# The low parts of a mixer's last weight tiles on VectorE alone

## The chip, the cores and the metric

The kernel runs on one core of one Trainium2 chip. The metric is the device time of one execution in microseconds (us). In the names of the profile TensorE is PE (its weight loads PEld), VectorE is DVE, ScalarE is ACT, GpSimd is POOL and SyncE is SP.

## What is computed

Two blocks follow one another on a sequence of 256 tokens of width 1024 in float32: a first one of two layers (feed-forward, dilated attention or retention, feed-forward), and a second one, also of two layers, each of a mixer and an MLP. The change is in the mixer of the second block. Its end, and what follows it, are:

```python
        gates = jax.nn.sigmoid((gate_logits + b_gate[l]).reshape(B, S, N_BRANCHES, D))
        merged = gates[:, :, 0] * y_diff + gates[:, :, 1] * y_mla + gates[:, :, 2] * y_mem
        x = x + merged @ w_out[l]

        u = rmsnorm(x, g_mlp[l]) @ w_mlp1[l]
        x = x + jnp.square(jax.nn.relu(u)) @ w_mlp2[l]
```

## The kernel before, in words

**Split products.** Every float32 product of activations and weights is made of three matmuls of rounded values: high by high, high by low, low by high. A weight tile is 128 x 1024 numbers. SP loads it from memory into one of four raw buffers (L1554), ScalarE copies it into one of four high buffers (`w_hi`, L1884), and then VectorE (L2186) or GpSimd (L2892) makes the low part, raw minus high (`w_lo`). TensorE waits for a tile's `w_lo` and then runs its 12 matmuls of 512 columns (`mm`, L1605 to L1607) or 24 of 256 columns (`mm_whole`, L1631, L1632, L1640).

**Order.** Python code writes one plan of steps, and each engine runs the steps that concern it in the plan's order, so every engine is a queue in order. When tile i has been used, `tile_used(i)` puts the step `split` of tile i + 4 into the plan. ScalarE's part of that step waits for TensorE's end of tile i, because it overwrites the same buffer. SP's part loads the tile that reuses the raw buffer, once the low part is made. Which engine makes the low part is decided when the step is written:

```python
    def split(self, i):
        self.step("split", i, "pool" if self.share and i % self.share == 0 else "dve")
```

`self.share` is 0 at the start of every stage. The mixer's step `outputs` sets it to 2 when attention begins (L1491), and the next stage, the MLP, sets it back to 0 (L663). In between, tiles with an even number have their low part made by GpSimd, the others by VectorE.

**The end of the mixer.** The last gated branches are added into `mx_merged` by VectorE (L2856, L2861: the merges). TensorE then transposes it (four groups of four, L1694), ScalarE copies the high part (`xt_hi`, L1914) and VectorE makes the low part (`xt_lo`, L2214). `last_plain` runs the output projection: eight tiles, four for columns 0 to 511 and four for columns 512 to 1023. They are called t0 to t7 here, and the first tiles of the MLP m0, m1 and so on. `hold_last` (L547) keeps back the split that t7's use would write, and those of the MLP's tiles behind it until `feed` releases them. So the steps `split` that are written while `last_plain` runs are those of t4, t5, t6, t7, m0, m1 and m2. The splits of t0 to t3 are written before it, in the merges.

**The start of the MLP.** Behind these steps `feed` (L675) writes for columns 0 to 511 and each half of the tokens: the addition of the projection to x (L2301, "add"), the product with the gain of the norm (`tok`, L2194, "gain"), and then the transposes of `tok` by TensorE, one group of four for each half ("turn", L1694). ScalarE's and VectorE's copies of them (`xt_hi`, `xt_lo`) feed the first matmuls of m0. The same for columns 512 to 1023 comes behind m0 and m1. POOL's next step then is the load of a gain (L2880).

Of the kernel before, what the change touches and what calls it, by code (L numbers as in the profile page):

```python
# [379 lines left out]
def drive(main, side=None, every=1, finish=True, steps=1):  # L380
    n = 0
    while True:
        try:
            next(main)
        except StopIteration as stop:
            result = stop.value
            break
        n += 1
        if side is not None and n % every == 0:
            for _ in range(steps):  # L390
                next(side, None)
    if side is not None and finish:
        for _ in side:
            pass
    return result


class Kernel:
# [869 lines left out]
    def mix(self, layer, _):  # L1268
# [252 lines left out]
        for c in range(2):  # L1521
            for half in range(HALVES):
                self.turn(lambda h, s: merged[:, h, s * P:(s + 1) * P], merged_t, half, [(4 * c + j, 4 * c + j) for j in range(4)],
                          [("merged", layer, half, c)], self.xt_after)
        self.tok_after = [[("turned", self.uid)]] * HALVES
        drive(self.last_plain(merged_t, a["w_out_2"][layer], D))


# [1519 lines left out]
```

## Time and profile before

| what | value |
|---|---|
| time before, median of 3 runs (lowest, highest) | 2466.48 us (2465.91, 2467.77) |
| profiled execution: its time | 2465.57 us |
| profiled execution: its span | 2464.3 us |
| TensorE clock granted, mean | 0.993 |
| busy: TensorE, VectorE, ScalarE, GpSimd | 97%, 62%, 48%, 12% |
| instructions | 34969 |

The span goes from the first to the last instruction of the profiled execution. Its time is 1.3 us longer, for what lies around the span, and 0.91 us below the median of the three runs. Busy shares are means over all ten stages. The first mixer ends near 1742 us of the span, the second near 2274 us.

### The profile page before, as it was taken

To read this page: it belongs to the slowest core of one execution; us is meant where nothing else is said; L and a number is where in the kernel's file an instruction comes from. 1 tells how busy PE (TensorE), PEld (TensorE's weight loads), DVE (VectorE), ACT (ScalarE), POOL (GpSimd) and SP (SyncE) were. 2 spreads that over 40 slices of the span, in tenths; PEclk is the share of its full clock that TensorE was granted. 3 is DMA by queue.
4 is the path that set the end of the run, shared out by engine and by line. 5 is a ranking of instruction groups with operands and counts; after the bars stand their busy time and mean duration, and the time that the engine had idled before them with its cause. 6 is when DMAs were issued, how large, how long until landed. Compare 5 with 4: busy or idle time off the path is not lost.

```text
span 2464.3 us, 34969 instructions
## 1 busy us (share of the span) xinstructions
PE 2385.3 (97%) x14214; PEld 2053.5 (83%) x14214; DVE 1522.5 (62%) x2325; ACT 1188.6 (48%) x1782; POOL 284.5 (12%) x247
## 2 busy tenths in 40 slices
PE   9998999889999999999999999999999999999999
PEld 8986777779979987777899787787898877887997
DVE  6555556666556547666665677755665577656654
ACT  4443454344435445444444464654554455554543
POOL 1100010000000000000000122333100122333000
PEclk9999999999999999999999999999999999999999
DMA  7755544446656655544566654445566554445564
GB/s 222 207 194 159 167 123 143 129 145 183 186 173 179 187 188 179 170 132 150 177 184 198 195 175 140 120 135 164 176 182 217 178 173 122 120 145 162 172 187 145
DMA packets 269424, 411.69 MB, mean 167 GB/s; under 512 B 13770, under 2 KB 141658, under 8 KB 269264
## 3 DMA queue, kind: packets, MB, share of 16 engines
q1 hardware_dynamic: 262400, 389.59, 52.1%
q0 software_dynamic: 6432, 19.28, 2.9%
q8 instruction: 112, 1.84, 0.3%
q10 hardware_dynamic: 432, 0.59, 0.1%
q14 instruction: 48, 0.39, 0.0%
HBM read 408.31 MB, written 1.10 MB: 166 GB/s over the span
## 4 chain that ended last, share of the span: by engine, by line
PE 79%; DVE 13%; ACT 5%; issue 2%; POOL 1%; DMA 0%; SPq 0%; ACTq 0%; DVEq 0%
PE banks L1605 14%; PE banks L1607 14%; PE banks L1606 14%; PE banks L1632 10%; PE banks L1631 9%; PE banks L1640 9%; DVE w_lo L2186 3%; ACT w_hi L1884 2%; PE banks L1754 1%; PE banks L1694 1%; PE banks L1707 1%; PE banks L1739 1%; DVE mx_merged L2861 1%; DVE probs L2373 1%; POOL stat L2873 1%
## 5 line engine op out<-in xcount | busy, mean ns | idle before, releaser
L2186 DVE TENSOR_TENSOR w_lo<-w_raw,w_hi 128x1024 fp32r<-128x1024 f32 x688 | 837.9, 1224 | 681.4 <-ACT w_hi L1884 678.9
L1884 ACT ACTIVATE w_hi<-w_raw 128x1024 fp32r<-128x1024 f32 (+2 forms) x744 | 776.8, 1049 | 564.3 <-PE banks L1607 413.6
L1631 PE MATMUL banks<-xt_hi,w_hi 128*128 128x256 f32 x1920 | 475.8, 282 | 12.1 <-ACT xt_hi L1914 8.9
L1632 PE MATMUL banks<-xt_hi,w_lo 128*128 128x256 f32 x1920 | 474.9, 286 | 0.0
L1605 PE MATMUL banks<-w_hi,xt_hi 128*128 128x512 f32 (+2 forms) x1088 | 447.3, 411 | 14.2 <-DVE xt_lo L2214 4.4
L1607 PE MATMUL banks<-w_hi,xt_lo 128*128 128x512 f32 (+2 forms) x1088 | 427.7, 393 | 0.0
L1606 PE MATMUL banks<-w_lo,xt_hi 128*128 128x512 f32 (+2 forms) x1088 | 427.3, 393 | 0.0
L1631 PEld LDWEIGHTS banks<-xt_hi,w_hi 128*128 128x128 f32 x1920 | 365.9, 191 | 15.9 <-issue 12.4
L1632 PEld LDWEIGHTS banks<-xt_hi,w_lo 128*128 128x128 f32 x1920 | 363.4, 189 | 0.0
L1640 PE MATMUL banks<-xt_lo,w_hi 128*128 128x256 f32 x1920 | 270.3, 283 | 0.0
L1605 PEld LDWEIGHTS banks<-w_hi,xt_hi 128*128 128x128 f32 x1088 | 206.7, 190 | 61.5 <-issue 8.1
L1640 PEld LDWEIGHTS banks<-xt_lo,w_hi 128*128 128x128 f32 x1920 | 248.6, 189 | 0.0
L1607 PEld LDWEIGHTS banks<-w_hi,xt_lo 128*128 128x128 f32 x1088 | 206.3, 190 | 47.4
L1606 PEld LDWEIGHTS banks<-w_lo,xt_hi 128*128 128x128 f32 x1088 | 206.8, 190 | 43.5 <-issue 3.1
L2873 POOL TENSOR_TENSOR stat<-stat,minus_half 128x1 f32<-128x1 f32 (+2 forms) x60 | 55.5, 931 | 1060.3 <-DVE stat L2273 712.0
L2892 POOL TENSOR_TENSOR w_lo<-w_raw,w_hi 128x1024 fp32r<-128x1024 f32 x56 | 134.5, 2401 | 277.2 <-ACT w_hi L1884 277.2
L1605 PE MATMUL banks<-w_hi,ffn_ht_hi 128*128 128x512 f32 x352 | 140.1, 398 | 0.0
L1607 PE MATMUL banks<-w_hi,ffn_ht_lo 128*128 128x512 f32 x352 | 139.1, 395 | 0.0
L1606 PE MATMUL banks<-w_lo,ffn_ht_hi 128*128 128x512 f32 x352 | 138.2, 393 | 0.0
L1607 PE MATMUL banks<-w_hi,mlp_ht_lo 128*128 128x512 f32 x256 | 101.7, 397 | 0.0
L1606 PE MATMUL banks<-w_lo,mlp_ht_hi 128*128 128x512 f32 x256 | 101.1, 395 | 0.0
L1605 PE MATMUL banks<-w_hi,mlp_ht_hi 128*128 128x512 f32 x256 | 100.9, 394 | 0.0
(398 smaller groups left out, 2824.7 us busy)
## 6 DMA issues: line engine op xcount, KB each, us to landing
w_raw<-in_w_mlp SPq DMA_DIRECT2D x128, 512.0 KB, 3.7
w_raw<-in_w_in SPq DMA_DIRECT2D x104, 512.0 KB, 3.7
w_raw<-in_ffn_w_gate SPq DMA_DIRECT2D x88, 512.0 KB, 4.1
w_raw<-in_ffn_w_up SPq DMA_DIRECT2D x88, 512.0 KB, 4.2
w_raw<-in_ffn_w_down SPq DMA_DIRECT2D x88, 512.0 KB, 3.6
w_raw<-in_attn_w_in SPq DMA_DIRECT2D x72, 512.0 KB, 3.8
w_raw<-in_ret_w_in SPq DMA_DIRECT2D x64, 512.0 KB, 3.9
w_raw<-in_ret_w_out SPq DMA_DIRECT2D x16, 512.0 KB, 3.9
```

Source lines behind the costliest of these rows:

```text
L1605: pe.matmul(bank, xh, wh, start=(c == 0), stop=False)
L1606: pe.matmul(bank, xh, wl, start=False, stop=False)
L1607: mm = pe.matmul(bank, xl, wh, start=False, stop=(c == b.chunks - 1))
L1631: pe.matmul(out[f], hi[:, cols], xh, start=(c == 0), stop=False)
L1632: pe.matmul(out[f], lo[:, cols], xh, start=False, stop=False)
L1640: mm = pe.matmul(out[f], hi[:, cols], xl, start=False, stop=(c == DC - 1))
L1694: mm = pe.transpose(bank[:, j * P:(j + 1) * P], t.src(t.half, s), order)
L1707: mm = pe.transpose(bank[0:z.shape[-1], at:at + P], z, order)
L1884: act.activation(k.w_hi[i % SPLIT][:, 0:m], k.raw[i % RAW][:, 0:m], ACT.Copy).then_inc(*ev.mark(k.w_hi_made, ("w_hi", i)))
L2186: dve.tensor_tensor(lo, raw, hi.bitcast(F32), ALU.subtract).then_inc(*ev.mark(k.w_lo_made, ("w_lo", i)))
L2873: pool.tensor_tensor(out, mean, k.minus_half[:, 0:n], ALU.pow).then_inc(*ev.mark(k.pool_done, name))
L2892: pool.tensor_tensor(lo, raw, hi.bitcast(F32), ALU.subtract).then_inc(*ev.mark(k.w_lo_pool, ("w_lo", i)))
```

## The change

The mixer sets `self.share` to 0 right before it calls `last_plain`, behind the steps of the merges and of the four transposes. The rest of the kernel is the same.

```diff
@@ -1523,6 +1523,7 @@
                 self.turn(lambda h, s: merged[:, h, s * P:(s + 1) * P], merged_t, half, [(4 * c + j, 4 * c + j) for j in range(4)],
                           [("merged", layer, half, c)], self.xt_after)
         self.tok_after = [[("turned", self.uid)]] * HALVES
+        self.share = 0
         drive(self.last_plain(merged_t, a["w_out_2"][layer], D))
```

## Rows read from the trace of the kernel before

**Rows 1.** The page, busy us, share and instructions of each engine

```profile
PE 2385.3 (97%) x14214; PEld 2053.5 (83%) x14214; DVE 1522.5 (62%) x2325; ACT 1188.6 (48%) x1782; POOL 284.5 (12%) x247
```

**Rows 2.** Windows of the first output projection: stretch, length, busy (instructions), clock, DMA, GB/s

```profile
1718.30:1730.00 11.70, 11.70 (x47) 9.43 (x46) 2.90 (x4) 3.78 (x4) 3.00 (x2) 0.89 0.21 59
1730.00:1742.00 12.00, 12.00 (x53) 9.62 (x52) 5.37 (x6) 4.25 (x4) 5.56 (x3) 1.00 0.63 196
```

**Rows 3.** Groups by line: low parts on GpSimd, and on VectorE by shape

```profile
L2892 POOL TENSOR_TENSOR w_lo<-w_raw,w_hi 128x1024 fp32r<-128x1024 f32 x56 | 134.5, 2401 | 277.2 <-ACT w_hi L1884 277.2
...
L2186 DVE TENSOR_TENSOR w_lo<-w_raw,w_hi 128x1024 fp32r<-128x1024 f32 x670 | 821.8, 1232 | 664.6 <-ACT w_hi L1884 662.1
```

**Rows 4.** Timeline of POOL (start, duration, what, idle before): t4, m2, second mixer's m2

```profile
1723.77 2.40 POOL L2892 TENSOR_TENSOR w_lo<-w_raw,w_hi 128x1024 fp32r<-128x1024 f32 x1 [10.61 <-ACT w_hi L1884]
...
1740.64 2.39 POOL L2892 TENSOR_TENSOR w_lo<-w_raw,w_hi 128x1024 fp32r<-128x1024 f32 x1 [3.21 <-ACT w_hi L1884]
...
2273.02 2.40 POOL L2892 TENSOR_TENSOR w_lo<-w_raw,w_hi 128x1024 fp32r<-128x1024 f32 x1 [3.22 <-ACT w_hi L1884]
```

**Rows 5.** Timeline of ACT: high parts of m1 and m2

```profile
1736.69 1.06 ACT L1884 ACTIVATE w_hi<-w_raw 128x1024 fp32r<-128x1024 f32 x1 [1.74 <-PE banks L1607]
1739.50 1.06 ACT L1884 ACTIVATE w_hi<-w_raw 128x1024 fp32r<-128x1024 f32 x1 [1.75 <-PE banks L1607]
```

**Rows 6.** Timeline of DVE at the joint of mixer and MLP (last row: second mixer)

```profile
1737.78 1.23 DVE L2186 TENSOR_TENSOR w_lo<-w_raw,w_hi 128x1024 fp32r<-128x1024 f32 x1 [4.40 <-ACT w_hi L1884]
1738.93 0.68 DVE L2301 TENSOR_TENSOR x<-banks,x 128x512 f32<-128x512 f32 x1
1739.64 0.69 DVE L2194 TENSOR_TENSOR tok<-x,gain 128x512 f32<-128x512 f32 x1
1740.25 0.69 DVE L2301 TENSOR_TENSOR x<-banks,x 128x512 f32<-128x512 f32 x1
1740.97 2.60 DVE L2194 TENSOR_TENSOR tok<-x,gain 128x512 f32<-128x512 f32 x1
...
1746.28 0.69 DVE L2194 TENSOR_TENSOR tok<-x,gain 128x512 f32<-128x512 f32 x1
...
2273.36 2.61 DVE L2194 TENSOR_TENSOR tok<-x,gain 128x512 f32<-128x512 f32 x1
```

**Rows 7.** Timeline of PE at the same joint: two turns and the first matmul of m0

```profile
1742.06 0.60 PE L1694 MATMUL banks<-ident,tok 128*128 128x128 f32 x4
1743.63 0.66 PE L1694 MATMUL banks<-ident,tok 128*128 128x128 f32 x4 [0.98 <-DVE tok L2194]
1745.07 0.36 PE L1631 MATMUL banks<-xt_hi,w_hi 128*128 128x256 f32 x1 [0.78 <-ACT xt_hi L1914]
```

**Rows 8.** Timelines in the merges: POOL's low part, and the merge beside it

```profile
1699.57 2.40 POOL L2892 TENSOR_TENSOR w_lo<-w_raw,w_hi 128x1024 fp32r<-128x1024 f32 x1 [3.15 <-ACT w_hi L1884]
...
1699.91 2.61 DVE L2861 TENSOR_TENSOR mx_merged<-mx_merged,tmp 128x512 f32<-128x512 f32 x1
```

**Rows 9.** PE's waits from 1752 us to 1850 us: total, times, longest

```profile
PE banks L1631 <- ACT xt_hi L1914: 0.8, 1, 0.8
```

**Rows 10.** Joints of feed-forward stages, PE's timeline, a window, and m0's 13th matmul

```profile
725.72 2.42 PE L1683 MATMUL banks<-causal,ident 128*128 128x384 f32 x7
731.64 0.55 PE L1631 MATMUL banks<-xt_hi,w_hi 128*128 128x256 f32 x1 [0.78 <-ACT xt_hi L1914]
...
734.34 0.34 PE L1631 MATMUL banks<-xt_hi,w_hi 128*128 128x256 f32 x1
...
731.00:734.40 3.40, 2.76 (x13) 2.79 (x14) 2.80 (x5) 1.44 (x2) 0.00 (x0) 0.51 0.03 6
...
1194.00 3.39 PE L1683 MATMUL banks<-causal,ident 128*128 128x384 f32 x10
...
1201.44 0.36 PE L1631 MATMUL banks<-xt_hi,w_hi 128*128 128x256 f32 x1 [0.78 <-ACT xt_hi L1914]
...
1746.57 0.29 PE L1631 MATMUL banks<-xt_hi,w_hi 128*128 128x256 f32 x1
```

## The prediction

> **What bounds the kernel.** I read the page first: TensorE is busy 97% of the span and nothing else comes near [rows 1]. So a change counts only where TensorE waits, or begins to. Next the windows of the output projection, where the change acts: TensorE is busy for the whole of both stretches, 23.7 us on end [rows 2]. There it waits for no weight tile, whoever makes the low parts. Then the timelines at the joint of mixer and MLP, and these matter. TensorE starts the first turn at 1742.06 right behind its last projection matmul, the second at 1743.63 behind a wait of 0.98 us for VectorE's gain, and the first matmul of m0 at 1745.07 behind a wait of 0.78 us for ScalarE's copy [rows 7]. VectorE is therefore on the critical path at this one place: its queue there is m1's low part, add, gain, add, gain, and the last gain takes 2.60 us where the same instruction takes 0.69 us a little later [rows 6]. Last, what comes behind: from 1752 us on TensorE waits once in 98 us, 0.8 us for the next turns' copies [rows 9], and from 2284 us to the end it also waits once, for as long. A delay at the joint has no slack behind it to vanish in.
>
> **What the change moves.** Seven splits are written in each output projection: t4, t5, t6, t7, m0, m1, m2. POOL's timeline has four low parts there, starting at 1723.77, then every 5.6 us up to 1740.64 [rows 4]: t4, t6, m0, m2. The second mixer has four likewise, the last at 2273.02. So 8 instructions of 2401 ns leave GpSimd (of 56) and 8 of 1232 ns come to VectorE [rows 3]: 9.9 us more for VectorE, 19.2 us less for GpSimd, neither of which is time by itself.
>
> **t4, t6, m0: nothing.** VectorE waits 4.40 us ahead of m1's low part [rows 6], and similarly ahead of the others, so 1.23 us fits in each time. The cover is TensorE's run of four tiles between a tile's high part and its use. t4's low part lands at 1726.17 today and is wanted 4.0 us later (eight tiles take 1718.3 to 1742.06, 2.97 us each, so t4 is used from about 1730.2). On VectorE it lands some 1.2 us earlier. Without that cover each would be worth at most that 1.2 us. SP's loads wait for low parts: those of m0, m2, m4 and m6 are issued about 1.2 us earlier. TensorE waited for no load, so I price this at nothing. POOL's own queue gets shorter; its next step, a gain's load, waits for VectorE's last gain and moves with it.
>
> **m2: the one that matters.** In VectorE's queue its low part stands ahead of add, gain, add, gain, and VectorE cannot pass it. It waits for m2's high part, which ScalarE starts at 1739.50 when TensorE ends t6 [rows 5]. From m1: high part starts at 1736.69, VectorE's low part at 1737.78, 1.09 us later; the add behind it starts 1.15 us after that [rows 5, 6]. So m2's low part starts at 1739.50 + 1.09 = 1740.59 and the first add at 1741.74, not at 1738.93: 2.81 us later. That is the delay of VectorE's queue, and the upper bound for TensorE's at one joint.
>
> Against it stands what GpSimd's instruction costs today. The last gain starts at 1740.97 and ends at 1743.57, 0.54 us after GpSimd's low part ends (1740.64 + 2.39 = 1743.03) [rows 4, 6]. The merges show the same pairing: a VectorE instruction that reads two tensors of SBUF, started beside a GpSimd low part, takes 2.61 us and ends 0.54 us after it [rows 8]. Two more merges of the same mixer repeat it. So 2.60 - 0.69 = 1.91 us of that gain is waiting for GpSimd, and it goes, because no GpSimd instruction is left there. Were the 2.60 us the gain's own, they would stay: the third rival.
>
> New times: first gain starts 1741.74 + 0.71 = 1742.45 and ends 1743.14; second add at 1743.06; second gain at 1743.78 (the spacing of [rows 6]: 0.71, 0.61, 0.72), ending 1743.78 + 0.69 = 1744.47. Before it ended at 1743.57: 2.81 - 1.91 = **0.90 us later**. The first turn starts at about 1743.2 instead of 1742.06 and is over by 1743.8, ahead of the second; it costs nothing more. The second turn starts near 1744.53, m0 at 1745.97. All behind keeps its distances: the adds and gains of the second columns, the release of m3, the turns behind m1 (0.90 us later too, like TensorE itself). m2's low part is ready 1.2 us earlier, and TensorE wants it only behind m0 and m1.
>
> **The longer gap in TensorE's work.** From the first turn's start to m0 lie 3.01 us now, with the clock at 2.4 GHz behind them: m0's 13th matmul starts 1.50 us after its first (1745.07 to 1746.57) [rows 7, 10]. From the last projection matmul's end to m0 there will be 3.9 us, with eight transposes in them. Two other joints, each with two turns in the gap, bound what that does. At 731 us the gap is 3.50 us, from the fill matmuls' end at 725.72 + 2.42 = 728.14 to 731.64. The granted clock behind it is 0.51, the 1.2 GHz level, and the 13th matmul starts 2.70 us after the first. At 1201 us the gap is 4.05 us (1194.00 + 3.39 = 1197.39 to 1201.44) and the first matmul takes 0.36 us like m0's today, so the clock held [rows 7, 10]. The price of a fall is 2.70 - 1.50 = 1.20 us at a joint, that of no fall 0. I take 0, since the joint nearest in length, 4.05 us, held; 1.20 us goes into the range.
>
> The Trainium skill (TensorE: Matmul & The Clock Gate, "Part 4: PE-mode transpose") says that the full clock does not engage for transposes, which speaks against this change: the new gap holds nothing else. By that rule the clock falls at both joints and the sum is + 4.2 us; by the row at 1201 us, + 1.8 us. The joint at 731 us agrees with the rule and the one at 1201 us does not.
>
> **Sum.** 0 for six instructions, + 0.90 us for each of the two m2. The second mixer has the same gain of 2.61 us beside the same GpSimd instruction [rows 4, 6]. Together **+ 1.8 us**. Bounds: below, - 0.9 us a joint, if VectorE's queue lost nothing and only the lock went (the second turn could follow the first at 1742.7, 0.9 us before 1743.63); above, + 2.81 us a joint. I take 0.90 because both its parts are read at this very joint. On the profiled execution: 2465.57 + 1.8 = 2467.4 us. The median of runs stands 0.91 us above it: 2466.48 + 1.8 = **2468.3 us**.
>
> A measurement of this kernel tells about 0.2% from no change, 4.9 us: faster means under 2461.6, slower over 2471.4.
>
> **Rivals.**
> 1. *The clock falls at one joint.* The gap grows from 3.0 to 3.9 us, and the two rows above stand on either side of the question [rows 10]. 2468.3 + 1.2 = 2469.5 us. It shows as a granted clock of about 0.5 behind the joint.
> 2. *It falls at both*, because transposes alone do not hold it. 731 us speaks for it, 1201 us against. 2468.3 + 2.4 = 2470.7 us. This is the case of the Trainium skill's page TensorE: Matmul & The Clock Gate.
> 3. *Slower.* The long gain is not GpSimd's doing but its own or the place's, and stays at 2.60 us. Then nothing sets off the 2.81 us: 5.6 us in all, 2472.1 us. It decides at VectorE's second gain: over 2 us long, this rival; 0.69 us, not. The short gain at 1746.28 and the pairing in the merges speak against it.
> 4. *No change.* The diff does not reach m2 (its split written elsewhere, GpSimd still starting at 1740.6), or the later gain is off TensorE's path by something I don't see. 2466.5 us. The count of GpSimd's low parts, 48 or more, decides.
> 5. *Gain.* Only the lock goes, - 0.9 us a joint: 2464.7 us. It would need VectorE to run add and gain ahead of m2, which its order forbids.
>
> **How the numbers follow.** Forecast (both joints + 0.9, clock holds) 0.62; rival 1 0.13; rival 2 0.08; rival 3 0.03; rival 4 0.10; rival 5 0.02; another disturbance 0.02. The three runs of before spread over 1.9 us, so each case has about 1 us on both sides. From 2466.2 to 2471.0 us lie the forecast, rivals 1 and 2 nearly whole and part of rival 4; outside are rivals 3 and 5. Faster by over 0.2% has no mechanism: 0.01. Slower holds rival 3 and the tail of rival 2: 0.05. The rest, 0.94, is within 0.2%.
>
> **What would show it.** GpSimd has 48 low parts, VectorE 8 more. At 1740.6 VectorE makes m2's low part, and add, gain, add, gain follow from 1741.7 with both gains at 0.7 us. The first turn starts near 1743.2 behind a wait for VectorE, the second near 1744.5, m0 near 1746.0; the second joint repeats it. The clock behind each joint is 1.00. I am wrong if m0 starts within 0.3 us of 1745.07, if the second gain is still long, or if the first 12 steps of m0 take 2.7 us and not 1.5 us.

## The result, and the profile after

| | kernel before | changed kernel |
|---|---|---|
| median of 20 executions each (us) | 2467.02 | 2470.64 |
| lowest, highest (us) | 2464.21, 2470.01 | 2468.3, 2474.99 |
| profiled execution: time, span (us) | 2465.57, 2464.3 | 2470.72, 2469.4 |
| its mean granted clock | 0.993 | 0.990 |

The ratio is 1.0014, with a 95% interval of 1.0008 to 1.002. The change costs 3.6 us by the medians: slower, clear of noise, and within the 0.2% that were called no change. The forecast was + 1.8 us, 2468.3 us. It stood on 2466.48 us, the median of the first three runs of the kernel before; over the 20 executions here that median is 2467.02 us, so 0.5 us of the 2.3 us by which 2468.3 missed lies in the base.

**What moved.** The page of the changed kernel, busy times:

```profile
PE 2391.0 (97%) x14214; PEld 2058.3 (83%) x14214; DVE 1528.7 (62%) x2333; ACT 1188.4 (48%) x1782; POOL 264.9 (11%) x239
```

and the two groups of low parts by shape:

```profile
L2187 DVE TENSOR_TENSOR w_lo<-w_raw,w_hi 128x1024 fp32r<-128x1024 f32 x678 | 831.7, 1232 | 660.9 <-ACT w_hi L1885 658.3
L2893 POOL TENSOR_TENSOR w_lo<-w_raw,w_hi 128x1024 fp32r<-128x1024 f32 x48 | 115.2, 2399 | 236.7 <-ACT w_hi L1885 236.6
```

Eight low parts changed engine, at the same price each [rows 3]. (One line was added, so the line numbers behind it are higher by one.)

**The joint of the first mixer and its MLP**, VectorE's timeline in the changed kernel (start, duration, what, idle before):

```profile
1736.96 1.22 DVE L2187 TENSOR_TENSOR w_lo<-w_raw,w_hi 128x1024 fp32r<-128x1024 f32 x1 [1.59 <-ACT w_hi L1885]
1739.77 1.23 DVE L2187 TENSOR_TENSOR w_lo<-w_raw,w_hi 128x1024 fp32r<-128x1024 f32 x1 [1.58 <-ACT w_hi L1885]
1740.91 0.68 DVE L2302 TENSOR_TENSOR x<-banks,x 128x512 f32<-128x512 f32 x1
1741.62 0.69 DVE L2195 TENSOR_TENSOR tok<-x,gain 128x512 f32<-128x512 f32 x1
1742.24 0.68 DVE L2302 TENSOR_TENSOR x<-banks,x 128x512 f32<-128x512 f32 x1
1742.95 0.69 DVE L2195 TENSOR_TENSOR tok<-x,gain 128x512 f32<-128x512 f32 x1
```

and TensorE's, the start of the last projection matmul in the kernel before, then the changed kernel from the same matmul on:

```profile
1741.82 0.39 PE L1607 MATMUL banks<-w_hi,xt_lo 128*128 128x512 f32 x1
```

```profile
1740.99 0.40 PE L1608 MATMUL banks<-w_hi,xt_lo 128*128 128x512 f32 x1
1742.37 0.66 PE L1695 MATMUL banks<-ident,tok 128*128 128x128 f32 x4 [0.98 <-DVE tok L2195]
1743.70 0.66 PE L1695 MATMUL banks<-ident,tok 128*128 128x128 f32 x4 [0.67 <-DVE tok L2195]
1745.14 0.36 PE L1632 MATMUL banks<-xt_hi,w_hi 128*128 128x256 f32 x1 [0.78 <-ACT xt_hi L1915]
```

This is to be read against [rows 6, 7]. "The joint" means here the time from the start of the last projection matmul to the first matmul of m0. m2's low part (1739.77) stands ahead of the adds. Counted from the last projection matmul, the first add starts 2.81 us later than before (0.08 us ahead of it, where it was 2.89 us ahead). The second gain takes 0.69 us, not 2.60. TensorE has a wait of 0.98 us ahead of the first turn, where it had none. The joint takes 1745.14 - 1740.99 = 4.15 us; before it took 1745.07 - 1741.82 = 3.25 us. That is 0.90 us, as worked out. The absolute times hide it: this execution reached the joint 0.83 us earlier. 0.65 us of that is its projection, 22.85 us from first to last matmul against 23.50, because the clock was low for a shorter part of it.

**The joint of the second mixer**, TensorE's timeline, the last projection matmul and m0's first and 13th:

```profile
2275.89 0.39 PE L1608 MATMUL banks<-w_hi,xt_lo 128*128 128x512 f32 x1
...
2280.09 0.55 PE L1632 MATMUL banks<-xt_hi,w_hi 128*128 128x256 f32 x1 [0.78 <-ACT xt_hi L1915]
2282.79 0.41 PE L1632 MATMUL banks<-xt_hi,w_hi 128*128 128x256 f32 x1
```

and ScalarE's, the copies of the turns of the second columns at the first and at the second joint:

```profile
1751.60 1.09 ACT L1915 ACTIVATE xt_hi<-banks 128x512 fp32r<-128x512 f32 x2 [5.66 <-PE banks L1695]
...
2289.10 1.09 ACT L1915 ACTIVATE xt_hi<-banks 128x512 fp32r<-128x512 f32 x2 [8.21 <-PE banks L1695]
```

Windows of the changed kernel behind both joints (length, busy and instructions of PE, PEld, DVE, ACT, POOL, then the granted clock):

```profile
1745.14:1748.10 2.96, 2.96 (x25) 2.96 (x26) 2.89 (x5) 0.80 (x1) 0.00 (x0) 1.00 0.02 6
...
2280.09:2285.80 5.71, 5.71 (x27) 5.71 (x28) 4.30 (x6) 0.81 (x1) 0.00 (x0) 0.50 0.03 7
```

This joint takes 4.20 us, against 3.26 in the kernel before. Here the clock fell to the 1.2 GHz level behind the lengthened gap (called a fall below): the granted clock is 0.50. From m0 to the copies of the second columns it takes 9.01 us, against 6.46 us at the first joint: 2.55 us lost. So the 5.1 us between the two spans are 1.8 us of delay at the joints and 2.5 us of the clock at the second joint. The rest, 0.7 us, was not taken apart; falls elsewhere differ between the two executions too. One of these stands at 1958 us, in code the change does not touch, first in the changed kernel, then in the kernel before:

```profile
1958.00:1961.60 3.60, 3.60 (x14) 3.60 (x13) 1.79 (x8) 3.48 (x9) 1.10 (x2) 0.53 0.15 55
```

```profile
1958.00:1961.60 3.60, 3.60 (x22) 3.60 (x22) 1.78 (x8) 3.48 (x9) 1.10 (x2) 1.00 0.12 45
```

### The profile page after: what moved, and what is told of

Same layout as the page of the kernel before. It is cut to its first block, busy times and chain, and to the rows that moved or that the text cites. A ratio compares the mean times of both kernels' runs of the same rounds, so it can differ in the third digit from the quotient of the medians.

```text
span 2469.4 us, 34969 instructions
## 1 busy us (share of the span) xinstructions
PE 2391.0 (97%) x14214; PEld 2058.3 (83%) x14214; DVE 1528.7 (62%) x2333; ACT 1188.4 (48%) x1782; POOL 264.9 (11%) x239
## 4 chain that ended last, share of the span: by engine, by line
PE 79%; DVE 13%; ACT 5%; issue 2%; POOL 1%; DMA 0%; ACTq 0%; DVEq 0%
PE banks L1606 14%; PE banks L1608 14%; PE banks L1607 14%; PE banks L1633 9%; PE banks L1632 9%; PE banks L1641 9%; DVE w_lo L2187 3%; ACT w_hi L1885 2%; PE banks L1755 1%; PE banks L1695 1%; PE banks L1708 1%; PE banks L1740 1%; DVE mx_merged L2862 1%; DVE probs L2374 1%; POOL stat L2874 1%
## 5 line engine op out<-in xcount | busy, mean ns | idle before, releaser
L2187 DVE TENSOR_TENSOR w_lo<-w_raw,w_hi 128x1024 fp32r<-128x1024 f32 (+1 forms) x696 | 847.9, 1224 | 677.7 <-ACT w_hi L1885 675.1
L1632 PEld LDWEIGHTS banks<-xt_hi,w_hi 128*128 128x128 f32 x1920 | 365.5, 190 | 15.7 <-issue 12.5
L2893 POOL TENSOR_TENSOR w_lo<-w_raw,w_hi 128x1024 fp32r<-128x1024 f32 x48 | 115.2, 2399 | 236.7 <-ACT w_hi L1885 236.6
```

What stands on the lines that cost most here:

```text
L1632: pe.matmul(out[f], hi[:, cols], xh, start=(c == 0), stop=False)
L2187: dve.tensor_tensor(lo, raw, hi.bitcast(F32), ALU.subtract).then_inc(*ev.mark(k.w_lo_made, ("w_lo", i)))
L2893: pool.tensor_tensor(lo, raw, hi.bitcast(F32), ALU.subtract).then_inc(*ev.mark(k.w_lo_pool, ("w_lo", i)))
```

## The experiments

A single profile can't tell the delay from the clock, since the clock differs between executions of one kernel. Every execution comes with its mean granted clock, though, to three digits. In 67 executions of the kernel before, taken beside the experiments (mean 2467.65 us, mean clock 0.9914), a line through time over clock has a slope of 1.65 us for 0.001. The last column below is the mean distance of a kernel's executions from that line, with its standard error: what is left of the difference at equal clock. The line takes a loss of clock to cost the same in every kernel. That is an assumption, but the five kernels with a joint of 4.14 or 4.15 us bear it out: they stand 1.6 to 1.9 us above the line, at mean clocks from 0.9904 to 0.9927. The joint is the first one.

| kernel | median us (n) | ratio to before, interval | mean clock | joint us | at equal clock us |
|---|---|---|---|---|---|
| changed | 2470.64 (20) | 1.0014, 1.0008 to 1.002 | 0.9904 | 4.15 | + 1.8 ± 0.2 |
| m2 alone moved | 2470.37 (11) | 1.0012, 1.0003 to 1.0021 | 0.9908 | 4.14 | + 1.9 ± 0.3 |
| all but m2 moved | 2468.8 (11) | 0.9997, 0.9988 to 1.0006 | 0.9917 | 3.24 | - 0.2 ± 0.3 |
| m2 behind the gains | 2464.34 (11) | 0.9989, 0.998 to 0.9998 | 0.9915 | 2.09 | - 3.0 ± 0.3 |
| changed, one fill | 2468.1 (11) | 1.0005, 0.9996 to 1.0014 | 0.9919 | 4.14 | + 1.7 ± 0.2 |
| changed, two fills | 2466.82 (11) | 0.9999, 0.999 to 1.0008 | 0.9927 | 4.14 | + 1.8 ± 0.2 |
| share ends at the cross merge | 2470.49 (12) | 1.0011, 1.0002 to 1.002 | 0.9908 | 4.14 | + 1.6 ± 0.4 |
| no GpSimd, m2 behind | 2479.55 (5) | 1.0042, 1.003 to 1.0054 | 0.9894 | 2.10 | + 7.9 ± 0.3 |
| t3 and m2 behind | 2459.63 (5) | 0.9966, 0.9954 to 0.9978 | 0.9924 | 2.10 | - 5.9 ± 0.4 |
| the same, share kept | 2461.32 (7) | 0.9971, 0.9961 to 0.9981 | 0.9920 | 2.11 | - 5.0 ± 0.2 |
| t1, t3 and m2 behind | 2454.96 (5) | 0.995, 0.9938 to 0.9963 | 0.9940 | 2.09 | - 8.3 ± 0.4 |

### m2 alone, and all but m2

The first is the kernel before with one low part per mixer moved, the second the changed kernel with that one moved back:

```diff
-        self.step("split", i, "pool" if self.share and i % self.share == 0 else "dve")
+        self.step("split", i, "pool" if self.share and i % self.share == 0 and i != self.apart else "dve")
...
+        self.apart = len(self.tiles) + 10
         drive(self.last_plain(merged_t, a["w_out_2"][layer], D))
```

```diff
-        self.step("split", i, "pool" if self.share and i % self.share == 0 else "dve")
+        self.step("split", i, "pool" if i == self.apart or self.share and i % self.share == 0 else "dve")
```

> The kernel before, with the low part of m2 alone given to VectorE in each mixer; t4, t6 and m0 stay with GpSimd. Theory (m2's place in VectorE's queue, less the lock, and the clock behind the longer gap): all of the change's delay is here. At the joint VectorE's second gain takes 0.7 us and ends about 0.9 us later relative to the last projection matmul, m0 starts 3.9 us behind the last projection matmul's start of the first turn before (3.0 us then), time about 1.8 us over the kernel before plus 1.2 us or more for each joint with a fall of the clock: 2468 to 2471 us, as the changed kernel. Rival (the six other low parts cost the time, through VectorE or the loads): time as before, 2467 us, joints at 3.0 us.

> The changed kernel, with the low part of m2 alone given back to GpSimd; t4, t6 and m0 on VectorE. Theory: as before, 2467 us: the second gain takes 2.6 us again beside GpSimd's low part, m0 starts 3.0 us behind the first turn, which follows the last projection matmul without a gap, and the clock holds at both joints. Rival (the other six): 2469 to 2471 us.

With m2 alone moved the time is the changed kernel's, in median, in joint and at equal clock. With all but m2 moved it is the kernel before's: ratio 0.9997, and - 0.2 ± 0.3 us at equal clock. (Its median misleads. Its executions fall into two groups, five from 2462.8 to 2465.7 us and six from 2468.8 to 2470.2 us; their mean, 2466.9 us, is 0.7 us under that of the kernel before in the same comparison.) So t4, t6 and m0, with the loads that they let start earlier, cost nothing that can be seen here. VectorE's timeline with all but m2 moved, then POOL's: the long gain is back beside the one GpSimd low part that is left there, and only there. (That a VectorE instruction stands still beside a GpSimd low part is what the prediction calls the lock.)

```profile
1735.34 1.23 DVE L2189 TENSOR_TENSOR w_lo<-w_raw,w_hi 128x1024 fp32r<-128x1024 f32 x1 [1.59 <-ACT w_hi L1887]
1736.48 0.68 DVE L2304 TENSOR_TENSOR x<-banks,x 128x512 f32<-128x512 f32 x1
1737.19 0.69 DVE L2197 TENSOR_TENSOR tok<-x,gain 128x512 f32<-128x512 f32 x1
...
1738.52 2.60 DVE L2197 TENSOR_TENSOR tok<-x,gain 128x512 f32<-128x512 f32 x1
```

```profile
1738.19 2.37 POOL L2895 TENSOR_TENSOR w_lo<-w_raw,w_hi 128x1024 fp32r<-128x1024 f32 x1 [27.64 <-ACT w_hi L1887]
```

The gain ends at 1741.12, 0.56 us after GpSimd's 1740.56. The third rival (the gain is long by itself) is out. The expectation was wrong in one point: it had the clock hold at both joints. In this kernel, whose gap is the kernel before's, it fell behind the first joint. The windows, the gap and what follows:

```profile
1739.60:1742.60 3.00, 1.26 (x9) 0.80 (x8) 2.22 (x3) 1.33 (x3) 0.96 (x1) 1.00 0.27 69
1742.60:1746.00 3.40, 3.39 (x16) 3.40 (x17) 3.33 (x6) 0.81 (x1) 0.00 (x0) 0.50 0.30 102
```

So a fall at the joint is not the change's own; the profile of the kernel before happened to have none.

The 12 profiles together show more than each alone. At the joints of 4.14 to 4.20 us in the kernels without a fill between the turns the clock fell at 4 of 8, one in each of four profiles; at those of 3.24 to 3.26 us at 1 of 4; at those of 2.09 to 2.11 us at 0 of 10. Where it fell at a long joint, the projection ahead had taken 23.67 to 24.30 us, with its clock low for longer at the start; where it held, 22.85 to 22.97 us. So a fall at the joint goes with what the clock did before it. No run sets that on purpose: it is a pattern and not a cause shown.

### m2's split behind the gains

```diff
             if c:
-                self.hold_last(rows * BLOCK // (P * TILE))
+                self.hold_last(rows * BLOCK // (P * TILE) - self.behind)
...
         part(1, 0)
+        self.release(self.behind)
+        self.behind = 0
...
+        self.behind = 1
         drive(self.last_plain(merged_t, a["w_out_2"][layer], D))
```

> The changed kernel, with m2's split placed behind add, gain, add, gain of the first columns in every queue; VectorE still makes all low parts. Theory: neither the 2.81 us of the queue nor the 1.91 us of the lock. The second gain ends 0.4 us before the last projection matmul, the second turn follows the first at once, m0 starts about 2.0 us behind the first turn's start (3.0 before, 3.9 changed): 1.0 us a joint less than before, 1.9 less than changed, and no fall of the clock at the joint. 2465 us against 2467 before and 2470.6 changed. If instead VectorE's own load were the trouble: as changed, 2469 to 2471 us.

2464.34 us, 6.3 us less than the changed kernel and faster than the kernel before (0.9989, interval 0.998 to 0.9998). VectorE makes exactly as many low parts as in the changed kernel (678); one in each mixer stands four instructions later in its queue. (The step moves in ScalarE's and SP's queues too.) VectorE's timeline, then TensorE's:

```profile
1741.34 1.23 DVE L2191 TENSOR_TENSOR w_lo<-w_raw,w_hi 128x1024 fp32r<-128x1024 f32 x1 [1.58 <-ACT w_hi L1889]
1742.48 0.68 DVE L2306 TENSOR_TENSOR x<-banks,x 128x512 f32<-128x512 f32 x1
...
1744.53 0.69 DVE L2199 TENSOR_TENSOR tok<-x,gain 128x512 f32<-128x512 f32 x1
1745.14 1.22 DVE L2191 TENSOR_TENSOR w_lo<-w_raw,w_hi 128x1024 fp32r<-128x1024 f32 x1
```

```profile
1745.38 0.39 PE L1612 MATMUL banks<-w_hi,xt_lo 128*128 128x512 f32 x1
1745.61 1.04 PE L1699 MATMUL banks<-ident,tok 128*128 128x128 f32 x8
1747.47 0.36 PE L1636 MATMUL banks<-xt_hi,w_hi 128*128 128x256 f32 x1 [0.83 <-ACT xt_hi L1919]
```

Both gains are over when the last projection matmul ends, and the eight transposes run as one piece. The joint is 2.09 us, 1.16 less than before. Twice that is 2.3 us of the 3.0 ± 0.3 us at equal clock; the other 0.7 us were not traced.

### One fill, and two, in the gap

A fill is a step of matmuls whose result nothing reads; it only gives TensorE work where it would wait.

```diff
         self.xt_after = [self.last_tile()]
+        if self.stages[st][0] == "mix":
+            self.step("fill", ("plain", st), 1)
...
             turned(0, 0)
+            if st and self.stages[st - 1][0] == "mix":
+                self.step("fill", ("between", st), 1)
```

(The first addition alone is the kernel with one fill.)

> The changed kernel with one fill matmul (two passes, 0.34 us each) on TensorE between the last projection matmul and the first turn, where it waits 1.1 us for the gain in the changed kernel: it adds work and delays nothing. Theory of the clock: the granted clock stays at 1.00 behind both joints in this and nearly every execution, so the time is the kernel before plus 1.8 us, 2468.8 us, 1 to 2 us less than the changed kernel, with a smaller spread. Rival (the clock has no part in the 3.6 us; the delay at a joint is larger than 0.9 us): same time as the changed kernel, 2470.6 us.

> The changed kernel with a fill ahead of the first turn and one between the two turns, where TensorE waits 0.67 us. With one fill the mean over executions was 2468.5 us at a mean clock of 0.9919, against 2470.9 us and 0.9905 for the changed kernel. Theory: the second fill (0.68 us) just fits or delays the second turn by 0.1 us; the clock holds at both joints in the profiled execution, 13th matmul of m0 1.5 us behind the first; 2468 to 2468.8 us. Rival (fills don't hold the clock, the earlier run was chance): the clock falls at some joint again and the time is 2469.5 to 2470.9 us.

The fills move neither the second turn nor m0 (the joint stays 4.14 us), and at equal clock both kernels stay where the changed one is, at + 1.7 and + 1.8 us. What they change is the mean clock: 0.9904 without, 0.9919 with one, 0.9927 with two, and the median falls by 2.5 and 3.8 us. Since the fills stand at the two joints and nowhere else, this is the evidence that falls at the joints cost part of the 3.6 us. The expectation for one fill was right in time and wrong in the profile: the clock still fell behind the first joint. With two fills it holds behind both, and behind projections of 24.29 and 23.65 us, about as long as those behind which it fell without them. TensorE's timeline of the first joint with two fills, and the window behind the second:

```profile
1743.78 0.81 PE L1688 MATMUL banks<-causal,ident 128*128 128x384 f32 x2
1744.94 0.66 PE L1699 MATMUL banks<-ident,tok 128*128 128x128 f32 x4 [0.35 <-DVE tok L2199]
1745.43 0.81 PE L1688 MATMUL banks<-causal,ident 128*128 128x384 f32 x2
1746.26 0.66 PE L1699 MATMUL banks<-ident,tok 128*128 128x128 f32 x4
1747.69 0.36 PE L1636 MATMUL banks<-xt_hi,w_hi 128*128 128x256 f32 x1 [0.78 <-ACT xt_hi L1919]
```

```profile
2282.80:2286.00 3.20, 3.20 (x29) 3.20 (x28) 2.48 (x4) 0.00 (x0) 0.00 (x0) 1.00 0.02 5
```

2466.82 us, below the expected 2468, is the kernel before's time: two fills give back in clock what the change costs in delay. They do not repair it.

### GpSimd's share ended earlier, and never begun

```diff
+            self.share = 0
             yield from merge(1, 2, mc_t, "w_cross_o_2", CROSS_H * CROSS_D, 4)
```

> The changed kernel, but GpSimd's share ends before the cross branch's merge, so the last two merges have no low part of GpSimd beside them either; m2's place as in the changed kernel. Theory (a place in VectorE's queue decides, the lock costs only where it stands last): the 1.9 us that three merge additions lose to the lock go, but the last merges still stand behind the low part of t3, whose high part waits for the last merge tile. First turn of the merged tile to first projection matmul stays at 6.1 us, the joint stays at 4.15 us, time as the changed kernel, 2470 us. Rival (the lock bounds the merges): that stretch shrinks by 1 to 2 us a mixer, 2467 us.

As expected: 2470.49 us. The three additions of the merges that took 2.2 to 2.8 us are 0.69 us each, and nothing is won. VectorE's timeline shows why: the last merges begin when t3's low part (1711.96) is made, and that waits for ScalarE's high part.

```profile
1710.16 1.22 DVE L2188 TENSOR_TENSOR w_lo<-w_raw,w_hi 128x1024 fp32r<-128x1024 f32 x1
1711.96 1.23 DVE L2188 TENSOR_TENSOR w_lo<-w_raw,w_hi 128x1024 fp32r<-128x1024 f32 x1 [0.58 <-ACT w_hi L1886]
1713.10 0.69 DVE L2858 TENSOR_TENSOR tmp<-banks,mx_gate 128x512 f32<-128x512 f32 x1
1713.82 0.69 DVE L2863 TENSOR_TENSOR mx_merged<-mx_merged,tmp 128x512 f32<-128x512 f32 x1
```

The next one has `self.share = 0` in the place of 2 at L1491, and m2 behind:

> GpSimd makes no low part at all in the mixers, and m2's split stands behind add, gain, add, gain. Theory: the joint is 2.1 us as with m2 behind, but VectorE has 40 more low parts of 1.2 us in attention, where it makes the row maxima that ScalarE and TensorE wait for; some reach TensorE: 2464.5 us plus 2 to 15 us. Rival (GpSimd's share is worth nothing anywhere once the order is right): 2464.5 us.

2479.55 us, 15 us over the kernel with m2 behind: at the upper end of what was expected. (VectorE makes 48 more low parts than there, not 40 as the expectation has it.) At equal clock 10.9 us of it are left. From 1500 us to the first merged turn it takes 223.4 us and not 214.9: TensorE is idle for 11.7 us in place of 7.6, and busy for 211.8 in place of 207.3 at a granted clock of 0.98 in place of 1.00. So GpSimd's share is worth much in attention, about half of it in waits and half in clock in that execution. Which wait grew was not settled; TensorE's waits by group show only 2.3 us more for the row maxima in both mixers.

### The other place of the same kind

t3's split, too, stands ahead of merges that don't need it. It was put behind the four turns of the merged tile, with m2's behind the gains and the share ended at the cross merge:

```diff
+                if (n, c) == (2, 1):
+                    self.hold_last(rows * BLOCK // (P * TILE))
                 b = yield from self.block(xt, a[name][layer], rows, c0, m, first)
...
         self.tok_after = [[("turned", self.uid)]] * HALVES
+        self.release()
         self.share = 0
```

> Both places mended: m2's split behind add, gain, add, gain, and t3's split behind the last merges and the four turns of the merged tile, with GpSimd's share ending before the cross branch's merge. Theory: the last merges no longer wait for t3's high part (1.06 us) and low part (1.2 us) nor for the lock, so the fourth turn starts about 1.6 us behind the first instead of 5.4 us, and the first projection matmul about 2.5 us behind it instead of 6.1 us: 3.6 us a mixer, 7 us in all, and perhaps 1.2 us a mixer more where the clock no longer falls there. Joint 2.1 us. 2464.3 - 7 = 2457 us, or 2455 us with the clock. Rival (VectorE's load bounds the merges and not the place of t3): 2464 us.

The kernel of the next run lacks both lines `self.share = 0`:

> Both places mended as in the run before, but GpSimd keeps its share to the end of the mixer, as in the kernel before: m2's and t2's low parts are GpSimd's. Theory: the lock comes back at both places. At the joint GpSimd's m2 starts ahead of the second gain, which takes 2.6 us again: joint 3.25 us. At the merges t2's low part holds up one addition by up to 1.9 us. 2 to 6 us over the run before: 2459 to 2463 us. Rival (with the right order it doesn't matter who makes them): as the run before.

2459.63 us, 0.9966 of the kernel before. The stretch from the first merged turn to the first projection matmul went from 6.16 us to 4.17, not to 2.5: the expectation had the lock and t3 but not t1, behind which the first columns' merges stood. With the share kept it is 5.01 us and the time 2461.32 us. That run's expectation failed at the joint, which was 2.11 us and not 3.25: `release` writes m2's split in the MLP's stage, where the share is 0 anyway, so VectorE made it. What is left between the two at the merges is 0.84 us in the first mixer and 0.77 in the second. It is put down to the lock on the merge additions, less the low part of t2 that VectorE is spared; the two were not taken apart.

The last step puts t1's split behind the first columns' merges as well:

```diff
-                if (n, c) == (2, 1):
+                if n == 2:
                     self.hold_last(rows * BLOCK // (P * TILE))
...
+                if (n, c) == (2, 0):
+                    self.release()
```

> As the run with both places mended, and t1's split also behind the merges of the first columns. In that run VectorE had no idle time from 1706.9 us to the last merge, because the first columns' merges stood behind t1's low part. Theory (place in the queue, not load): the first columns' merges start up to 2 us earlier, the last merges about 1.0 us earlier (1.1 us for t2's low part is still ahead of them), and the first projection matmul comes 3.1 us behind the first turn instead of 4.17 us: 1 us a mixer, 2457.6 us against 2459.6. Rival (VectorE's load is the bound there): 4.17 us and 2459.6 us as it was.

2454.96 us, 0.995 of the kernel before (0.9938 to 0.9963) and 15.7 us under the changed kernel's 2470.64, the fastest of all. TensorE's timeline of the merged turns and the first projection matmul:

```profile
1710.14 1.03 PE L1705 MATMUL banks<-ident,mx_merged 128*128 128x128 f32 x8
1711.62 0.66 PE L1705 MATMUL banks<-ident,mx_merged 128*128 128x128 f32 x4 [0.44 <-DVE mx_merged L2872]
1712.94 0.66 PE L1705 MATMUL banks<-ident,mx_merged 128*128 128x128 f32 x4 [0.67 <-DVE mx_merged L2872]
1713.64 0.47 PE L1616 MATMUL banks<-w_hi,xt_hi 128*128 128x512 f32 x1
```

3.50 us where 3.1 were expected, and yet 2.6 us better than expected: in this execution the clock did not fall there in either mixer, as the first projection matmul's 0.47 us (0.77 in the kernel with two splits behind) already shows. The projection takes 22.3 us of TensorE from first to last matmul and not 23.7. At equal clock the step from two splits to three is worth 2.4 us (8.3 - 5.9), where 2 us were expected.

## Why the prediction was right, and what it missed

**Eight low parts move; six cost nothing.** Right, and shown: with all but m2 moved the time is the kernel before's, - 0.2 ± 0.3 us at equal clock.

**+ 2.81 us of queue, - 1.91 us of lock, + 0.90 us at each joint.** Right to 0.01 us in the trace of the first joint (3.25 to 4.15 us), to 0.04 us in that of the second (3.26 to 4.20), and at equal clock + 1.8 ± 0.2 us, the sum that was forecast. m2 alone does it. That the lock was GpSimd's doing is shown by giving m2 back.

**The clock.** This term was mis-sized: it was put at 0, and measured 1.5 us. So the forecast's centre, + 1.8 us, is half of what was measured, and the median fell into the range because the range left room for falls. The step reads "The price of a fall is 2.70 - 1.50 = 1.20 us at a joint, that of no fall 0. I take 0, since the joint nearest in length, 4.05 us, held". It treated a fall as a property of a gap, and read it from one profile. The other profiles have the same two joints, in code that no run touches, and both come out differently in most of them. The joint near 731 us (gap 3.5 us) fell in 2 of 12, the one near 1201 us (4.05 us) in 10 of 12, and in each profile exactly one of the two. This is the one near 1201 us in the changed kernel, m0's first and 13th matmul, then the window:

```profile
1200.16 0.36 PE L1632 MATMUL banks<-xt_hi,w_hi 128*128 128x256 f32 x1 [0.78 <-ACT xt_hi L1915]
...
1202.62 0.41 PE L1632 MATMUL banks<-xt_hi,w_hi 128*128 128x256 f32 x1
...
1200.16:1203.50 3.34, 3.34 (x17) 3.34 (x18) 3.27 (x6) 0.80 (x1) 0.00 (x0) 0.54 0.00 0
```

The first matmul takes 0.36 us, and yet the 13th comes 2.46 us behind it at a granted clock of 0.54. So a first matmul of 0.36 us does not show that the clock held, which was the prediction's reason at 1201 us (there the 13th, at 1.52 us, bears the reading out). The joint that the 0 was taken from is one at which the clock mostly falls.

The mean clock shows the size: 0.9904 against 0.9914, which at 1.65 us for 0.001 is 1.5 us. 1.8 + 1.5 = 3.3 us is the distance between the means (2470.92 and 2467.65), by the way the line splits it; the medians lie 3.6 us apart. That a longer gap raises how often the clock falls there fits the fills and the counts above (1 of 4, 4 of 8), but these are too few to show it. The price of one fall was too low too: 1.20 us counts the first 12 steps, and the fall goes on beyond them. Up to the turns of the second columns it cost 1.4 to 1.5 us at four of the joints, and 2.55 us at the changed kernel's second.

Of the prediction's three signs of being wrong two came up in the changed kernel's profile. The first 12 steps of m0 took 2.70 us at the second joint, where the clock was not 1.00: that is the clock term. And m0 started at 1745.14, within 0.3 us of 1745.07: that sign misled, because it was an absolute time and the projection ahead had been 0.65 us shorter. On the base of the 20 executions, 2467.02 us, the first two rivals (a fall at one joint, at both) stand at 2470.0 and 2471.2 us, and the median, 2470.64 us, lies between them.

**The rule on transposes.** By the Trainium skill's rule (TensorE: Matmul & The Clock Gate, "Part 4: PE-mode transpose"), as the prediction read it, both joints would fall, + 4.2 us. The changed kernel's profile has one fall of two and m2 alone's likewise, and the transposes themselves ran at a granted clock of 1.00 where the joint held, so read as "always" it is not borne out. Fills in the gap raised the mean clock; but they also filled idle time, so no run here tells whether it is the transposes or the waits that let the clock fall.

**No slack behind the joint.** Right: the delay arrives whole at the end.

## What to carry to other kernels

On an engine that runs in order, ask not only whether it has the time for an instruction, but what the instruction waits for and who stands behind it. One low part of 1.2 us cost 2.8 us of queue because it waited for data that came late; placed four instructions further back it cost nothing that can be seen, and placing three such in each mixer, with GpSimd's share ended at the cross merge, gave 12.7 us between the means (2467.65 - 2454.95), 8.3 us of it at equal clock. Where TensorE's gaps change by a microsecond, compare many executions by time and mean clock together, before a difference of a few microseconds is given to one cause. A fall or a hold that one profile shows at a gap is one draw: look at the same place in other profiles before it becomes a term of a sum.

## What the runs showed of the hardware

VectorE's instructions of 128x512 with two tensors in SBUF (gain, merge addition) ended 0.54 to 0.56 us after a GpSimd low part that had started before them, in each pair looked at. In the kernel before, four low parts of 128x1024 that VectorE made beside one took 1.33 to 1.99 us in place of 1.23 and ended 1.07 to 1.09 us after it: in each case nearly the instruction's own length, as if it began when GpSimd ended. The profile counts the standstill as busy. An add that reads one tensor from PSUM kept its 0.68 us beside it. The granted clock of one and the same kernel differed between executions by up to 0.005 in the mean (0.989 to 0.994 in 67 executions), and that goes with 8 us of time. A fall can begin a few matmuls behind the gap: near 1201 us m0's first matmul took 0.36 us and those from the third on 0.41 us, at a granted clock of 0.54.
